# Other SBUF start addresses, modulo 512 bytes, for the stationary operands of a split-fp32 transformer kernel

## The chip, the cores and the metric

The kernel runs on one core of one Trainium2 chip. The metric is the device time of one execution in microseconds (us); lower is better. Times given for a kernel are the median of several executions with their lowest and highest.

## What is computed

The reference runs two transformer blocks, one after the other, on 256 tokens of width 1024, all in fp32. The first block normalises x, projects it; of the columns q, k and v go to a differential attention of 8 heads, u to a causal depthwise convolution of 31 taps, and g to two gates; then it has an FFN with 2816 inner columns. The second block has a stick-breaking attention, a linear recurrence and an FFN with 4096 inner columns. Cut to the dense products, which are what the change is about:

```python
# first block
proj = rms_norm(x, attn_norm_w) @ w_in                    # 1024 x 7168: q, k, v, u, g
y_a = attention(q, k, v) @ w_proj_attn                    # 1024 x 1024
y_b = silu(layer_norm(conv(u))) @ w_proj_conv             # 1024 x 1024
x = x + (g_a * y_a + g_b * y_b) @ w_out                   # 1024 x 1024
gt, up = split(rms_norm(x, ffn_norm_w) @ w_gate_up)       # 1024 x 5632
x = x + (silu(gt) * up) @ w_down                          # 2816 x 1024
# second block
proj = rms_norm(x, norm1_g_2) @ w_in_2                    # 1024 x 2560
x = x + concat(attention_2, lru) @ w_out_2                # 1024 x 1024
x = x + square(relu(rms_norm(x, norm2_g_2) @ w_up_2)) @ w_down_2   # 1024 x 4096, 4096 x 1024
```

## The kernel before, in words

**Numbers in two parts.** Every dense product is made of three matmuls. A weight w and an activation x are each kept as a high part (fp32r, the format in which TensorE reads it in one pass) and a low part (what the high part leaves): x_hi·w_hi + x_hi·w_lo + x_lo·w_hi. The activation part is the stationary operand (128 x 128: 128 rows of the contraction, 128 tokens), the weight part is the moving one (128 x 512).

**Units.** All weights are cut into units of four row blocks of 128 by 512 columns (1 MB), 120 of them (two have only two row blocks), in the fixed order of `weight_chunks`. For each unit SyncE's queue loads `raw` (three buffers, L428, or L409 for the first two), ScalarE copies it to `w_hi` (L589, L594), and VectorE (L928, L933) or, for units 7 to 27, GpSimd (L574) writes `w_lo` = raw - w_hi. `w_hi` and `w_lo` have three buffers each. TensorE then runs the unit, one row block j after the other and for each the two token tiles t, with these three matmuls (L1640, L1641, L1642; in the very last unit L1625 to L1627 with the loops turned round):

```python
x_h = hi[:, k0 + j, P * t:P * (t + 1)]
x_l = lo[:, k0 + j, P * t:P * (t + 1)]
nc.tensor.matmul(o, x_h, w_hi[:, slot, j, :], start=begin_, stop=False)
nc.tensor.matmul(o, x_h, w_lo[:, slot, j, :], start=False, stop=False)
mm = nc.tensor.matmul(o, x_l, w_hi[:, slot, j, :], start=False, stop=end_)
```

A unit is 4 x 2 x 3 = 24 such matmuls. `parts(c)` picks the stationary pair: `h_hi, h_lo` for the products that read a normalised x (and for `w_proj_conv`), `y_hi, y_lo` for `w_proj_attn`, `w_out` and `w_out_2`, `m_hi, m_lo` for the two down projections. The order of the work is written out by hand: small work of TensorE (transposes through `turn`, L1325; attention scores, L1370 and L1403; probabilities times v, L1387; suffix sums, L1414 to L1418; recurrence gates, L1439 and L1440) is put between units or in the middle of one. VectorE also runs the 31-tap convolution (L972) in the first 200 us.

**Places in SBUF.** Buffers are laid out by hand with `place` and `sb` (L152 to L160), at byte offsets in each partition. `w_hi` and `w_lo` take 24,576 bytes each, `h_hi` and `h_lo` 8,192, `m_hi` and `m_lo` 32,768. `y_hi` and `y_lo` lie on `m_hi`'s memory, and so do `gates` and `x_in` behind them (L217); `m_lo` and the first block's working buffers share the region behind `m_hi`. Slices inside a weight buffer step by 2,048 bytes, and the stationary slices by 512 (t) and 1,024 (j). All these sizes are multiples of 512, and so, in the kernel before, each of the six activation parts and each slice of them starts at the same address modulo 512 bytes as each weight slice: a distance of 0. Counted from `w_hi`, modulo 512, other buffers start at: `q_t`, `k_t`, `v_tok`, `gates`, `x_in`, `q2_t`, `k2_t`, `ff_m`, `neg_tri` 0; `wr_g`, `wi_g`, `w2_t` 160; `lru_u` 64; `raw`, `conv`, `x_res`, `ln_r` 64; `ident` and `mean_w` 192; `tok` 320; `a_tok`, `probs_t`, `glu` 448.

Of the kernel before, what the change touches and what calls it, by code (L numbers as in the profile page):

```python
# [9 lines left out]
F32R = mybir.dt.float32r  # L10
# [4 lines left out]
P = 128  # L15
D = 1024
S = 256
NT = S // P
EPS = 1e-6
KT = D // P  # L20
CW = 512
UK = 4
# [21 lines left out]
FK2 = FF2 // P  # L44
# [39 lines left out]
def build(nc, a, out):  # L84
# [19 lines left out]
    RAW, SPLIT = 3, 3  # L104
# [44 lines left out]
    with ExitStack() as ctx:  # L149
        cursor = [(nc.sbuf_base + 31) // 32 * 32]  # L150

        def place(name, shape, dt=F32, at=None):  # L152
            size = int(np.prod(shape[1:])) * 4
            if at is None:
                at = cursor[0]
                cursor[0] += (size + 31) // 32 * 32
            return nc.alloc_sbuf_tensor_at(name, shape, dt, offset=at), at

        def sb(name, shape, dt=F32, at=None):
            return place(name, shape, dt, at)[0]  # L160
# [2 lines left out]
            return ctx.enter_context(nc.semaphore(name))  # L163


        w_hi = sb("w_hi", [P, SPLIT, UK, CW], F32R)
        w_lo = sb("w_lo", [P, SPLIT, UK, CW], F32R)

        h_hi = sb("h_hi", [P, KT, S], F32R)
        h_lo = sb("h_lo", [P, KT, S], F32R)  # L170

        m_hi, m_at = place("m_hi", [P, FK2, S], F32R)
        y_hi, y_at = place("y_hi", [P, KT, S], F32R, at=m_at)
        qk_square = sb("qk_square", [P, NT, CW], at=y_at)
        y_lo = sb("y_lo", [P, KT, S], F32R, at=m_at + 4 * KT * S)

        region = cursor[0]
        m_lo = sb("m_lo", [P, FK2, S], F32R)
        ff_m = sb("ff_m", [P, NT, 256])
        ff_s = sb("ff_s", [P, NT, 256])  # L180
# [15 lines left out]
        glu_t, at = place("glu_t", [P, KT, PAD + S])  # L196
# [16 lines left out]
        ln_r, at = place("ln_r", [P, S])  # L213
        conv_sum = sb("conv_sum", [P, S], at=at)
        region_end = max(region_end, cursor[0])

        cursor[0] = m_at + 4 * (FK2 // 2) * S  # L217
        gates, x_at = place("gates", [P, NT, 2 * D])
        x_in = sb("x_in", [P, NT, D], at=x_at)
        vecs = sb("vecs", [VROWS, D], at=x_at + 4 * NT * D)  # L220
# [7 lines left out]
        x2_tok, at = place("x2_tok", [P, NT, W2])  # L228
# [17 lines left out]
        conv, at = place("conv", [P, KT, S])  # L246
# [1459 lines left out]
```

## Time and profile before

| | before |
|---|---|
| median of 3 executions | 742.98 us (742.23 to 743.13) |
| the profiled execution's own time | 745.36 us |
| its span, first to last instruction | 743.6 us |
| mean granted TensorE clock | 0.998 |
| TensorE matmuls, busy | 729.4 us (98%), 3428 of them |
| weight loads (beside the matmuls) | 594.2 us (80%) |
| VectorE / ScalarE / GpSimd busy | 483.9 / 398.1 / 174.6 us |
| DMA traffic | 131.45 MB, mean 177 GB/s |

The median is 2.4 us below the profiled execution's own time, and that is 1.8 us above its span. The busy time of TensorE counts each matmul from its start to a modelled end; matmuls overlap, so the distance from one start to the next, which the timeline shows, is what a matmul costs in a row of them.

### The profile page before, as it was taken

To read this page: it belongs to the slowest core of one execution; us is meant where nothing else is said; L and a number is where in the kernel's file an instruction comes from. 1 tells how busy PE (TensorE), PEld (TensorE's weight loads), DVE (VectorE), ACT (ScalarE), POOL (GpSimd) and SP (SyncE) were. 2 spreads that over 40 slices of the span, in tenths; PEclk is the share of its full clock that TensorE was granted. 3 is DMA by queue.
4 is the path that set the end of the run, shared out by engine and by line. 5 is a ranking of instruction groups with operands and counts; after the bars stand their busy time and mean duration, and the time that the engine had idled before them with its cause. 6 is when DMAs were issued, how large, how long until landed. Compare 5 with 4: busy or idle time off the path is not lost.

```text
span 743.6 us, 9120 instructions
## 1 busy us (share of the span) xinstructions
PE 729.4 (98%) x3428; PEld 594.2 (80%) x3428; DVE 483.9 (65%) x671; ACT 398.1 (54%) x526; POOL 174.6 (23%) x127
## 2 busy tenths in 40 slices
PE   7998999999999999999999999999999999999998
PEld 6786777777778888888888888888788888888886
DVE  4697988889987665555556454677866565653531
ACT  6744666655694464444445255569945555444330
POOL 1089799998310003000000000150001000000000
PEclk9999999999999999999999999999999999999999
DMA  8965445355547547566564555642354556455540
GB/s 287 258 208 183 126 159 197 115 199 169 170 154 265 181 137 227 171 188 200 178 186 170 196 198 170 227 130 97 114 177 164 177 170 207 170 182 192 203 142 29
DMA packets 82803, 131.45 MB, mean 177 GB/s; under 512 B 3988, under 2 KB 35804, under 8 KB 82760
## 3 DMA queue, kind: packets, MB, share of 16 engines
q1 hardware_dynamic: 82224, 129.61, 53.5%
q0 software_dynamic: 528, 1.25, 0.6%
q8 instruction: 28, 0.46, 0.3%
q14 instruction: 15, 0.12, 0.0%
q10 hardware_dynamic: 8, 0.02, 0.0%
HBM read 129.61 MB, written 1.25 MB: 176 GB/s over the span
## 4 chain that ended last, share of the span: by engine, by line
PE 70%; DVE 10%; POOL 9%; ACT 5%; issue 2%; DMA 2%; SPq 1%; ACTq 0%; POOLq 0%; DVEq 0%
PE acc L1640 21%; PE acc L1642 21%; PE acc L1641 21%; POOL w_lo L574 5%; DVE aux L972 5%; PE aux L1325 3%; DMA raw<-w_in_dram 2%; POOL qk_r L479 2%; ACT w_hi L589 1%; DVE w_lo L928 1%; POOL probs L546 1%; POOL qk_ss L491 1%; POOL probs L548 1%; DVE gates L1131 1%; SPq L409 0%
## 5 line engine op out<-in xcount | busy, mean ns | idle before, releaser
L928 DVE TENSOR_TENSOR w_lo<-raw,w_hi 128x2048 fp32r<-128x2048 f32 (+1 forms) x97 | 220.1, 2269 | 127.8 <-ACT w_hi L589 127.8
L589 ACT ACTIVATE w_hi<-raw 128x2048 fp32r<-128x2048 f32 x118 | 223.7, 1900 | 143.1 <-PE acc L1642 139.3
L1640 PE MATMUL acc<-w_hi,h_hi 128*128 128x512 f32 x640 | 257.5, 402 | 4.4 <-DVE tok L983 2.5
L1642 PE MATMUL acc<-w_hi,h_lo 128*128 128x512 f32 x640 | 251.2, 392 | 0.0
L1641 PE MATMUL acc<-w_lo,h_hi 128*128 128x512 f32 x640 | 250.4, 391 | 0.0
L1640 PEld LDWEIGHTS acc<-w_hi,h_hi 128*128 128x128 f32 x640 | 121.1, 189 | 30.6 <-DVE tok L983 3.1
L1642 PEld LDWEIGHTS acc<-w_hi,h_lo 128*128 128x128 f32 x640 | 120.7, 189 | 26.1
L1641 PEld LDWEIGHTS acc<-w_lo,h_hi 128*128 128x128 f32 x640 | 121.0, 189 | 23.2
L574 POOL TENSOR_TENSOR w_lo<-raw,w_hi 128x2048 fp32r<-128x2048 f32 x21 | 98.0, 4671 | 0.8 <-ACT w_hi L589 0.7
L972 DVE SCALAR_TENSOR_TENSOR aux<-glu_t,vec_t,aux 128x256 f32<-128x256 f32 x232 | 94.0, 481 | 0.0
L479 POOL TENSOR_TENSOR rstd<-ms,nhalf 128x2 f32<-128x2 f32 x4 | 8.7, 2183 | 339.9 <-DVE ms L955 339.9
L1640 PE MATMUL acc<-w_hi,m_hi 128*128 128x512 f32 x208 | 81.2, 390 | 0.0
L1642 PE MATMUL acc<-w_hi,m_lo 128*128 128x512 f32 x208 | 81.0, 389 | 0.0
L1641 PE MATMUL acc<-w_lo,m_hi 128*128 128x512 f32 x208 | 80.9, 389 | 0.0
L1640 PEld LDWEIGHTS acc<-w_hi,m_hi 128*128 128x128 f32 x208 | 39.0, 188 | 8.1
L1642 PEld LDWEIGHTS acc<-w_hi,m_lo 128*128 128x128 f32 x208 | 39.0, 188 | 8.1
L1641 PEld LDWEIGHTS acc<-w_lo,m_hi 128*128 128x128 f32 x208 | 39.0, 188 | 8.0
L616 ACT ACTIVATE m_hi<-aux 128x512 fp32r<-128x512 f32 x27 | 15.3, 598 | 54.5 <-PE aux L1325 54.5
L1640 PE MATMUL acc<-w_hi,y_hi 128*128 128x512 f32 x96 | 38.6, 402 | 0.9 <-DVE y_lo L1023 0.9
L1642 PE MATMUL acc<-w_hi,y_lo 128*128 128x512 f32 x96 | 37.5, 391 | 0.0
L1641 PE MATMUL acc<-w_lo,y_hi 128*128 128x512 f32 x96 | 37.4, 390 | 0.0
L947 DVE TENSOR_TENSOR m_lo<-aux,m_hi 128x512 fp32r<-128x512 f32 x27 | 17.9, 687 | 16.9 <-ACT m_hi L616 16.8
(219 smaller groups left out, 646.0 us busy)
## 6 DMA issues: line engine op xcount, KB each, us to landing
raw<-w_in_dram SPq DMA_DIRECT2D x30, 1024.0 KB, 5.2
raw<-w_down_dram SPq DMA_DIRECT2D x26, 1024.0 KB, 5.0
raw<-w_gate_up_dram SPq DMA_DIRECT2D x44, 512.0 KB, 4.8
raw<-w_up_dram SPq DMA_DIRECT2D x16, 1024.0 KB, 5.5
raw<-w_out_dram SPq DMA_DIRECT2D x8, 1024.0 KB, 5.0
raw<-w_in_dram SPq DMA_DIRECT2D x12, 512.0 KB, 4.6
raw<-w_proj_attn_dram SPq DMA_DIRECT2D x4, 1024.0 KB, 5.0
raw<-w_proj_conv_dram SPq DMA_DIRECT2D x4, 1024.0 KB, 5.1
```

Source lines behind the costliest of these rows:

```text
L479: nc.gpsimd.tensor_tensor(out_, in_, nhalf[:, 0:in_.shape[1]], ALU.pow).then_inc(s_out, 1)
L491: nc.gpsimd.tensor_scalar(part, part, 1.0 / HD, qk_e[:, st, t:t + 1], ALU.mult, ALU.add)\
L574: nc.gpsimd.tensor_tensor(w_lo[:, u % SPLIT, 0:nk, :], raw[:, u % RAW, 0:nk, :], f(w_hi[:, u % SPLIT, 0:nk, :]), ALU.subtract).then_inc(w_ ...
L589: nc.scalar.activation(w_hi[:, u % SPLIT, 0:nk, :], raw[:, u % RAW, 0:nk, :], ACT.Copy)\
L616: nc.scalar.activation(dst[:, 2 * g:2 * g + 2, :], aux[:, bank, :].rearrange("p (a b) -> p a b", a=2), ACT.Copy, scale=scale).then_inc(s_o ...
L928: nc.vector.tensor_tensor(w_lo[:, u % SPLIT, 0:nk, :], raw[:, u % RAW, 0:nk, :], f(w_hi[:, u % SPLIT, 0:nk, :]), ALU.subtract).then_inc(w_ ...
L947: nc.vector.tensor_tensor(lo[:, 2 * g:2 * g + 2, :], aux[:, bank, :].rearrange("p (a b) -> p a b", a=2), f(hi[:, 2 * g:2 * g + 2, :]), ALU ...
L972: nc.vector.scalar_tensor_tensor(out=conv_acc(ct) if tap < TAPS - 1 else conv[:, ct, :], in0=glu_t[:, ct, tap:tap + S], scalar=vcol(R_CONV ...
L1325: return nc.tensor.transpose(out_, in_, ident[:, :])
L1640: nc.tensor.matmul(o, x_h, w_hi[:, slot, j, :], start=begin_, stop=False)
L1641: nc.tensor.matmul(o, x_h, w_lo[:, slot, j, :], start=False, stop=False)
L1642: mm = nc.tensor.matmul(o, x_l, w_hi[:, slot, j, :], start=False, stop=end_)
```

## The change

The weights' parts stay where they are. Each of the six activation parts gets a start of its own modulo 512 bytes, counted from `w_hi`: `h_hi` 64, `h_lo` 256, `m_hi` 320, `y_hi` 384, `y_lo` 192, and `m_lo` 448 (it is the first buffer of the region). Gaps of less than 512 bytes are left between buffers. `gates`, `x_in`, `q2_t` and what lies with them now begin right behind `y_lo` (192). The region and all behind it move up by 960 bytes, so that, modulo 512, they stand 64 lower than before: `q_t`, `k_t`, `v_tok`, `ff_m` 448, `wr_g`, `w2_t` 96, `lru_u` 0, `raw`, `x_res`, `ln_r` 0, `ident` 128, `tok` 256, `a_tok`, `probs_t` 384. No instruction is added, removed or moved, and no wait changes.

```diff
-        w_hi = sb("w_hi", [P, SPLIT, UK, CW], F32R)
+        w_hi, w_at = place("w_hi", [P, SPLIT, UK, CW], F32R)
         w_lo = sb("w_lo", [P, SPLIT, UK, CW], F32R)
 
-        h_hi = sb("h_hi", [P, KT, S], F32R)
-        h_lo = sb("h_lo", [P, KT, S], F32R)
-
-        m_hi, m_at = place("m_hi", [P, FK2, S], F32R)
-        y_hi, y_at = place("y_hi", [P, KT, S], F32R, at=m_at)
+        def apart(at, off):
+            return at + (w_at + off - at) % 512
+
+        h_hi, at = place("h_hi", [P, KT, S], F32R, at=apart(cursor[0], 64))
+        h_lo, at = place("h_lo", [P, KT, S], F32R, at=apart(at + 4 * KT * S, 256))
+
+        m_hi, m_at = place("m_hi", [P, FK2, S], F32R, at=apart(at + 4 * KT * S, 320))
+        y_hi, y_at = place("y_hi", [P, KT, S], F32R, at=apart(m_at, 384))
         qk_square = sb("qk_square", [P, NT, CW], at=y_at)
-        y_lo = sb("y_lo", [P, KT, S], F32R, at=m_at + 4 * KT * S)
-
-        region = cursor[0]
+        y_lo, at = place("y_lo", [P, KT, S], F32R, at=apart(y_at + 4 * KT * S, 192))
+        gates_at = at + 4 * KT * S
+
+        region = apart(max(m_at + 4 * FK2 * S, gates_at + 4 * 2 * NT * D), 448)
+        cursor[0] = region
         m_lo = sb("m_lo", [P, FK2, S], F32R)
...
-        cursor[0] = m_at + 4 * (FK2 // 2) * S
+        cursor[0] = gates_at
         gates, x_at = place("gates", [P, NT, 2 * D])
```

## Rows read from the trace of the kernel before

**Rows 1.** The page: engines' busy time, and the granted clock by slices.

```profile
PE 729.4 (98%) x3428; PEld 594.2 (80%) x3428; DVE 483.9 (65%) x671; ACT 398.1 (54%) x526; POOL 174.6 (23%) x127
...
PEclk9999999999999999999999999999999999999999
```

**Rows 2.** Waits of TensorE and of the two splits; groups of instructions with idle time before.

```profile
PE acc L1640 <- DVE w_lo L928: 0.4, 1, 0.4
...
L589 ACT ACTIVATE w_hi<-raw 128x2048 fp32r<-128x2048 f32 x116 | 221.6, 1914 | 136.1 <-PE acc L1642 132.3 <-DMA raw<-w_in_dram 3.8
...
DVE w_lo L928 <- ACT w_hi L589: 127.8, 68, 5.1
```

**Rows 3.** Groups of TensorE's instructions: shapes, count | busy us, mean ns | idle.

```profile
L1640 PE MATMUL acc<-w_hi,h_hi 128*128 128x512 f32 x640 | 257.5, 402 | 4.4 <-DVE tok L983 2.5 <-DVE h_lo L941 1.5 <-DVE w_lo L928 0.4
...
L1640 PE MATMUL acc<-w_hi,m_hi 128*128 128x512 f32 x208 | 81.2, 390 | 0.0
...
L1640 PE MATMUL acc<-w_hi,y_hi 128*128 128x512 f32 x96 | 38.6, 402 | 0.9 <-DVE y_lo L1023 0.9
...
L1625 PE MATMUL acc<-w_hi,m_hi 128*128 128x512 f32 x8 | 3.1, 389 | 0.0
```

**Rows 4.** Timeline of TensorE, 48 matmuls in a row of the first down projection.

```profile
419.79 0.39 PE L1640 MATMUL acc<-w_hi,m_hi 128*128 128x512 f32 x1
...
430.45 0.39 PE L1642 MATMUL acc<-w_hi,m_lo 128*128 128x512 f32 x1
```

**Rows 5.** Timeline of TensorE behind a break, in the up projection.

```profile
599.51 0.47 PE L1640 MATMUL acc<-w_hi,h_hi 128*128 128x512 f32 x1
599.83 0.40 PE L1641 MATMUL acc<-w_lo,h_hi 128*128 128x512 f32 x1
...
600.30 0.39 PE L1640 MATMUL acc<-w_hi,h_hi 128*128 128x512 f32 x1
...
601.68 0.39 PE L1640 MATMUL acc<-w_hi,h_hi 128*128 128x512 f32 x1
```

**Rows 6.** Timeline of TensorE: gates of the recurrence and attention scores, plain fp32.

```profile
492.56 0.60 PE L1439 MATMUL aux<-lru_u,wr_g 128*128 128x256 f32 x2
...
495.58 0.59 PE L1440 MATMUL aux<-lru_u,wi_g 128*128 128x256 f32 x2
...
530.07 0.71 PE L1403 MATMUL aux<-q_t,k_t 64*128 64x256 f32 x4
530.61 0.39 PE L1405 MATMUL aux<-q_t,k_t 64*128 64x128 f32 x4
```

**Rows 7.** Groups of TensorE: three kinds of transposes.

```profile
L1325 PE MATMUL aux<-ident,tok 128*128 128x128 f32 x112 | 14.9, 275 | 1.0 <-DVE probs L1106 0.7 <-DVE tok L983 0.3
...
L1325 PE MATMUL aux<-ident,ff_m 128*128 128x128 f32 x44 | 6.6, 272 | 0.0
L1325 PE MATMUL aux<-ident,x_res 128*128 128x128 f32 x48 | 6.3, 273 | 0.2 <-DVE x_res L1159 0.2
```

**Rows 8.** Groups of weight loads (PEld).

```profile
L1640 PEld LDWEIGHTS acc<-w_hi,h_hi 128*128 128x128 f32 x640 | 121.1, 189 | 30.6 <-DVE tok L983 3.1 <-issue 2.1 <-DVE h_lo L941 1.9
...
L1440 PEld LDWEIGHTS aux<-lru_u,wi_g 128*128 128x128 f32 x8 | 1.5, 190 | 0.2
```

**Rows 9.** Groups of VectorE with two inputs in SBUF.

```profile
L928 DVE TENSOR_TENSOR w_lo<-raw,w_hi 128x2048 fp32r<-128x2048 f32 x95 | 217.6, 2291 | 123.3 <-ACT w_hi L589 123.3
...
L1246 DVE TENSOR_TENSOR h_lo<-conv,h_hi 128x1024 fp32r<-128x1024 f32 x2 | 2.4, 1222 | 0.8 <-ACT h_hi L868 0.8
L1019 DVE TENSOR_TENSOR conv<-conv,ln_r 128x1024 f32<-128x1024 f32 x2 | 2.4, 1218 | 0.0
```

**Rows 10.** Busy time by stretch: us, PE, PEld, DVE, ACT, POOL, clock, DMA share, GB/s.

```profile
100.00:200.00 100.00, 98.71 (x486) 76.97 (x485) 87.21 (x205) 61.19 (x131) 88.01 (x54) 1.00 0.51 167
...
600.00:700.00 100.00, 100.00 (x462) 83.09 (x462) 55.05 (x42) 45.43 (x39) 0.00 (x0) 1.00 0.55 189
```

**Rows 11.** Groups of TensorE, first 200 us alone.

```profile
L1640 PE MATMUL acc<-w_hi,h_hi 128*128 128x512 f32 x224 | 92.9, 415 | 4.4 <-DVE tok L983 2.5 <-DVE h_lo L941 1.5 <-DVE w_lo L928 0.4
```

## The prediction

> **What bounds the kernel now.** I read the page first: TensorE's matmuls are busy for 98% of the span, and its clock is granted in full in every slice [rows 1], so neither another engine nor the clock is the limit. Next the waits. TensorE's wait for the low part of the weights comes to 0.4 us in all; ScalarE, which makes the high part, waits 132.3 us for TensorE to give buffers back and only 3.8 us for transfers; VectorE waits 127.8 us for ScalarE [rows 2]. Whoever feeds TensorE is early. The groups of matmuls say what it does: 640 + 208 + 96 + 8 = 952 times the first of three matmuls with 512 columns, 1920, 648 and 288 of them on h, m and y, 2856 in all [rows 3]. Their mean of some 390 to 402 ns is a modelled length, so I took what one costs in a row from the timeline: 48 of them start between 419.79 and 430.45, which is 10.66 us over 47 steps, 226.8 ns each [rows 4]. 2856 x 226.8 ns is 647.7 us, 87% of the span of 743.6 us. The kernel is a stream of one kind of matmul, and the change can move the time by more than a microsecond or two only through this step.
>
> **Is there something in a step to win or lose?** Two views say that the step is not a constant of nature. Behind a break, the first step takes 320 ns (599.51 to 599.83), the next two together 0.47 us, so 235 ns each, and the eight from 599.83 to 601.68 on average 231 ns; only then does it settle [rows 5]. So the step depends on how one instruction stands in time to its neighbours. And plain fp32 matmuls, which run in two passes, go faster per pass: 14 steps from 492.56 to 495.58 are 215.7 ns each [rows 6], although each has its own weight load, as long as the others' (190 against 189 ns) [rows 8]. Between 226.8 and 215.7 lie 11.1 ns. In each step the array reads 512 elements of the moving part and meanwhile loads the next 128 x 128 stationary part. If these two readings disturb each other in SBUF, and if how much depends on their addresses modulo 512 bytes, then the change acts on 2856 steps. Before, the distance is 0 everywhere.
>
> **The change part by part.**
>
> *The instructions.* None is added, removed or moved, in no queue, SP's and GpSimd's included, and no wait is new. The edit costs what different addresses cost, and nothing else.
>
> *The 2856 matmuls.* No row of the trace has an fp32r matmul of 512 columns at another distance, so this price is bounded. Below, a step can fall to 215.7 ns: 2856 x 11.1 ns = 31.7 us less. Above, the slowest pair behind a break (235 ns) gives 8.2 ns more a step, 23.4 us more. Which value do the nearest rows speak for? The recurrence gates have their stationary part at 160 and their moving part at 64; the scores of the second attention have both at 0, the distance of the big matmuls. If a shared distance of 0 hurt, the scores should show it: their first four instructions (two pairs, the two of a pair on different halves of the rows) take 0.54 us from 530.07 to 530.61 [rows 6], and with 0.32 us for the first pair, the price of a first step behind a break [rows 5], the second pair takes 0.22 us, the gates' 215.7 ns within the last digit shown. The transposes have `ident` as the moving part at 192 and their stationary part at 320, 0 or 64; they take 275, 272 and 273 ns [rows 7]. Nothing here moves with the distance. These rows read the moving part at half the speed or for 128 columns only, so they don't settle it, but they are the only ones in which the distance varies. I take 0 for the change of a step.
>
> *The three steps of a break.* The eight steps behind a break cost 231 instead of 227 ns, some 35 ns, and the timeline has some 80 such breaks: 2.8 us in all. Another distance could lengthen or shorten this. Bounds: 2.8 us less to 2.8 us more; I take 0.
>
> *The split on ScalarE, VectorE and GpSimd.* `raw` goes from distance 64 to 0 against `w_hi`. Rows with two SBUF inputs exist at both distances: 1222 ns at 64 (`conv` and `h_hi`), 1218 ns at 0 (`conv` and `ln_r`), same size [rows 9]. So the 95 splits of 2291 ns on VectorE move by at most 4 ns per 1024 elements, 95 x 8 ns = 0.8 us of busy time. It costs the end nothing: VectorE idles 123.3 us before these splits [rows 9]. If that cover were gone the price would be this 0.8 us. The transfers into `raw` start 64 bytes from where they did, counted modulo 512; a slower one is hidden behind the 132.3 us that ScalarE waits for TensorE, and 3.8 us is all that it waits for transfers [rows 2]. Both cost 0.
>
> *Sum.* 745.4 us, the profiled execution's own time, plus 0 is 745.4 us; the median of the executions stands 2.4 us below that, so I forecast 743.0 us. An effect of 0.2%, 1.5 us, is about what a measurement of this kernel can tell from no change.
>
> One page of the notes speaks against the change. The Trainium skill, "TensorE: Matmul & The Clock Gate", in the part on what happens when a matmul is issued, says that TensorE reads moving and stationary operands through two independent SBUF ports, so that loading weights takes no reading speed from a running matmul. By that the addresses would not matter and the sum would be 743.0 us as well; by the bound of 215.7 ns it would be 711. The same page puts a warm step of 512 columns at N/2.4 + 2.5 ns, about 216 ns; the trace agrees for the plain fp32 passes and disagrees by 11 ns for the fp32r ones, so one of the two statements does not hold here.
>
> **The rivals.**
>
> *1. Faster: distance 0 is a collision.* Stationary and moving part begin at the same place modulo 512 in every step, and the moving stream is held up by the load. The new distances clear it. For it: 11.1 ns a step that the load alone doesn't explain, and a step that depends on relative timing behind a break [rows 4 to 6]. Against it: the scores at distance 0. Price by buffer: h, at 64 and 256, 1920 x 11.1 = 21.3 us; m, at 320 and 448, 648 x 11.1 = 7.2 us; y, at 384 and 192, 3.2 us. In the first 200 us lie 3 x 224 = 672 of h's [rows 11], 7.5 us, and there VectorE and GpSimd are 87% and 88% busy [rows 10]. The 14 us or so that each has free in 100 us would be enough for a gain of 4%, but the convolution is late next, and part may be lost. With all of it 743.0 - 31.7 = 711 us; with the early part lost 719 us; with y alone 740 us. Its middle is some 725 us.
>
> *2. Slower: a new distance settles at a longer step.* A step now ends in a favourable position, which it finds some eight steps behind a break. If the other distances never find it, each step stays at the 231 ns of the approach: 2856 x 4.2 ns = 12.0 us, 755 us; if it stays at the worst pair's, 766 us. It decides from a mean step above 227.3 ns on (1.5 us over 2856). For it: the steps of 231 and 235 ns in the timeline [rows 5]. Against it: these also happen at distance 0, so what sets them may not be the address.
>
> *3. The change doesn't do what it says.* All three matmuls of a triple have weight slices at 0, and `w_hi` and `w_lo` are the same distance from each other as before. If the conflict is one of successive moving reads, the homes of x, y and m don't touch it, and the time is 743.0 us. I count this with the forecast.
>
> **How the numbers follow.** Forecast, no effect, with rival 3 in it: 0.38; its own range is 741.5 to 744.5. Rival 1: 0.36, because 11 ns a step are there to be explained and the change touches every step. Rival 2: 0.26, because a position that is good by chance is as easily left. The likeliest case gives the time. For the range I add from the others until about 0.2 is left out: down to 718, which takes in rival 1 but for its full price, and up to 758, which takes in rival 2 with the 231 ns step (0.38 + some 0.28 + some 0.16). Faster by over 0.2%, 0.36; within 0.2%, 0.38; slower by over 0.2%, 0.26.
>
> **What would show it.** The timeline of the first down projection: 48 matmuls in 10.66 us means no effect; 10.14 us would be rival 1 in full, 10.86 us rival 2 at 231 ns. If only some distances matter, h, y and m will have different steps: read one stretch of each, and compare the step during which an h_lo (256) or m_lo (448) is loaded with the others of its triple. The length of VectorE's split should stay at 2291 ns within 10. The prediction is wrong if the step on h differs by more than 0.5 ns from 226.8, and wrong in its reason if the step is the same and the time moves all the same.

## The result and the profile after

The changed kernel takes 753.01 us (752.28 to 754.83, 3 executions) against 742.98 us before; the ratio is 1.0144, with a 95% interval of 1.0122 to 1.0166. It is slower by 10.0 us, or 1.4%.

The page of the changed kernel, the parts that answer to [rows 1] (all line numbers are 5 higher behind the edit: L1640 is now L1645):

```profile
span 753.1 us, 9120 instructions
...
PE 741.7 (98%) x3428; PEld 594.4 (79%) x3428; DVE 484.4 (64%) x671; ACT 398.1 (53%) x526; POOL 173.4 (23%) x127
...
PEclk9999999999999999999999999999999999999999
```

The same instructions, the same work on the other engines within 1.2 us each, the same clock in every slice, and 12.3 us more on TensorE (741.7 against 729.4). So the time went into the matmuls themselves. The groups that answer to [rows 3], and the split that answers to [rows 9]:

```profile
L1645 PE MATMUL acc<-w_hi,h_hi 128*128 128x512 f32 x640 | 260.1, 406 | 3.4 <-DVE tok L988 1.9
...
L1645 PE MATMUL acc<-w_hi,m_hi 128*128 128x512 f32 x208 | 82.0, 394 | 0.0
...
L1645 PE MATMUL acc<-w_hi,y_hi 128*128 128x512 f32 x96 | 39.3, 409 | 0.8 <-DVE y_lo L1028 0.8
```

```profile
L933 DVE TENSOR_TENSOR w_lo<-raw,w_hi 128x2048 fp32r<-128x2048 f32 x95 | 217.6, 2291 | 126.2 <-ACT w_hi L594 126.2
```

VectorE's split is unchanged to the nanosecond (2291 ns), though `raw` moved against `w_hi`. The timeline gives what a matmul costs in a row. Of the changed kernel, 96 steps of the first down projection, and 30 steps of the up projection:

```profile
407.28 0.39 PE L1645 MATMUL acc<-w_hi,m_hi 128*128 128x512 f32 x1
...
429.55 0.39 PE L1645 MATMUL acc<-w_hi,m_hi 128*128 128x512 f32 x1
...
608.79 0.40 PE L1645 MATMUL acc<-w_hi,h_hi 128*128 128x512 f32 x1
...
615.79 0.40 PE L1645 MATMUL acc<-w_hi,h_hi 128*128 128x512 f32 x1
```

22.27 us over 96 steps are 232.0 ns on m, and 7.00 us over 30 are 233.3 ns on h, where [rows 4] had 226.8. Note how little the other views show of this: no new wait, no gap, and a busy share of 98% both times. The mean of a group rises by 4 to 7 ns (402 to 406 on h, 390 to 394 on m, 402 to 409 on y), but it is a mean of modelled lengths; the distance between starts is what a step costs.

**Where the 9.5 us of span come from.** I paired the two traces matmul by matmul, since they have the same 3428 in the same order, and took the differences of the steps. Steps of ordinary length (under 260 ns) on h cost 8.7 us more, on m 3.3 and on y 1.3: 13.3 us. Three things give some of it back. Steps that contain a wait or follow a break are 1.6 us shorter, because a slower TensorE waits less for the others; the small matmuls are 0.8 us shorter; and one piece, 1.4 us, is an accident of this one execution's clock. The kernel before waits 2.5 us for `tok` in its early part, and behind it the granted clock is at 1.2 GHz for a moment. Busy times by stretch, the kernel before, then the changed one:

```profile
60.00:65.00 5.00, 5.00 (x18) 3.93 (x19) 5.00 (x14) 0.24 (x1) 5.00 (x2) 0.66 0.13 43
```

```profile
60.00:65.00 5.00, 4.60 (x24) 3.90 (x25) 5.00 (x14) 2.35 (x5) 4.99 (x3) 1.00 0.16 52
```

The column before the last two is the clock: 0.66 against 1.00. In the kernel before, seven matmuls there take some 427 ns, double the length; in the changed one the wait is 1.9 us and none of them does. A smaller piece goes the other way and is counted within the 1.6 us: at 10 us of the span, where the kernel before is at full speed, the changed kernel still has three steps of 0.42 to 0.58 us, and with the transposes beside them this costs it some 0.8 us. At the first product on y, which is at the end of the stretch in which VectorE and GpSimd are nearly full, the changed kernel is even ahead, by 0.7 us:

```profile
197.50 0.47 PE L1645 MATMUL acc<-w_hi,y_hi 128*128 128x512 f32 x1
```

(198.21 us before.) All of the net loss is made behind that point, where TensorE has hardly a wait: -0.7 + 10.2 us.

### The profile page after: what moved, and what is told of

Read it like the earlier page. It is cut to its first block, busy times and chain, and to the rows that moved or that the text cites. A ratio compares the mean times of both kernels' runs of the same rounds, so it can differ in the third digit from the quotient of the medians.

```text
span 753.1 us, 9120 instructions
## 1 busy us (share of the span) xinstructions
PE 741.7 (98%) x3428; PEld 594.4 (79%) x3428; DVE 484.4 (64%) x671; ACT 398.1 (53%) x526; POOL 173.4 (23%) x127
## 4 chain that ended last, share of the span: by engine, by line
PE 72%; DVE 12%; ACT 5%; POOL 5%; issue 2%; DMA 2%; SPq 1%; ACTq 0%; DVEq 0%; POOLq 0%
PE acc L1645 22%; PE acc L1647 22%; PE acc L1646 22%; DVE aux L977 7%; PE aux L1330 4%; DMA raw<-w_in_dram 2%; POOL w_lo L579 2%; POOL qk_r L484 2%; ACT w_hi L594 1%; DVE probs L1111 1%; POOL qk_ss L496 1%; DVE gates L1136 1%; DVE aux L973 1%; SPq L414 1%; DVE qk_ss L1129 0%
## 5 line engine op out<-in xcount | busy, mean ns | idle before, releaser
L1645 PE MATMUL acc<-w_hi,h_hi 128*128 128x512 f32 x640 | 260.1, 406 | 3.4 <-DVE tok L988 1.9
L1647 PE MATMUL acc<-w_hi,h_lo 128*128 128x512 f32 x640 | 253.9, 397 | 0.0
L1645 PEld LDWEIGHTS acc<-w_hi,h_hi 128*128 128x128 f32 x640 | 121.2, 189 | 31.8 <-DVE tok L988 2.3
L1645 PE MATMUL acc<-w_hi,m_hi 128*128 128x512 f32 x208 | 82.0, 394 | 0.0
L1645 PEld LDWEIGHTS acc<-w_hi,m_hi 128*128 128x128 f32 x208 | 39.2, 188 | 8.5
L1645 PE MATMUL acc<-w_hi,y_hi 128*128 128x512 f32 x96 | 39.3, 409 | 0.8 <-DVE y_lo L1028 0.8
```

## The experiments

Each is the changed kernel with other offsets or one line more. I name a distance as the kernel does, modulo 512 and counted from `w_hi`. For each run I give the settled step: the mean of all steps of 512 columns from the 13th of an unbroken stretch on, without those of 245 ns and more, taken from the trace for h, m and y. The kernel before has 226.8, 226.7 and 226.8 by this measure, the changed one 232.9, 231.9 and 233.4. With slightly other rules for what counts, the means of this and the other runs move by up to 0.4 ns on y, which has few such steps, and by 0.1 ns on h and m.

### Four theories of the cause

A: the distance between stationary and moving parts sets the step. B: what costs is that the high and the low part of a pair stand at different distances. C: the absolute addresses set it. D: the place of `raw` and of what lies behind it does.

**Uniform pairs, first set.**

```diff
-h_hi 64, h_lo 256, m_hi 320, m_lo 448, y_hi 384, y_lo 192
+h_hi 64, h_lo 64, m_hi 128, m_lo 128, y_hi 256, y_lo 256
```

> Both parts of each pair start at one and the same distance: h 64, m 128, y 256. Theory A (each load's distance from the moving weights sets the step): the step differs from 226.7 ns by buffer, each with its own value, and the time is not that of the kernel before. Theory B (what costs is that the high and the low part stand at different distances, so that successive loads jump): 226.7 ns for h, m and y and 743 us. Theories C (absolute addresses) and D (the place of raw and of the buffers behind it): some 233 ns everywhere, 753 us, if they explain the loss, since the rest lies about as after the change.

Measured: h 233.3, m 232.4, y 227.3 ns; 753.09 us, ratio 1.0143 (1.0128 to 1.0159). The mean on y holds some steps that are still settling; its stretches end at 226.7. B falls, since equal distances of a pair cost as much. D falls too, as the three buffers differ within one kernel while `raw` has one place. C is not settled here: it was expected to give one step everywhere, but the parts' absolute addresses differ between the buffers as much as their distances do.

**Uniform pairs, second set.**

```diff
-h_hi 64, h_lo 256, m_hi 320, m_lo 448, y_hi 384, y_lo 192
+h_hi 192, h_lo 192, m_hi 320, m_lo 320, y_hi 448, y_lo 448
```

> As the run before with other distances: h 192, m 320, y 448. Theory A: three more values of the step, one for each distance, different from one another. Theory B: 226.7 ns throughout, 743 us. C and D: as in the run before, the same step for all three buffers.

Measured: h 229.2, m 233.3, y 229.0 ns; 749.1 us, ratio 1.0084 (1.0067 to 1.0101). Three different values were expected; two came. By distance, so far: 192 and 448 agree, 64 and 320 agree, 256 is as good as 0. That the values repeat after 256 was not in any theory.

**Everything moved by 64 bytes.** All distances 0, as before the change:

```diff
-        cursor = [(nc.sbuf_base + 31) // 32 * 32]
+        cursor = [(nc.sbuf_base + 31) // 32 * 32 + 64]
```

> All buffers as in the kernel before, with distance 0, but everything moved up by 64 bytes, the weights too. Theories A, B and D: the step stays at 226.7 ns in the settled stretches and the time at 743 us. Theory C (absolute addresses modulo 512): the step changes, to some 233 ns.

Measured: 226.8, 226.7 and 226.8 ns; 741.53 us (one execution). The stationary parts stand here at the absolute addresses modulo 512 that h had in the first of these runs, and the step is the good one: C is out.

**The tail alone.** Distances 0, `raw` at 0 from the weights as in the changed kernel:

```diff
-        cursor[0] = region_end
+        cursor[0] = apart(region_end, 0)
         raw = sb("raw", [P, RAW, UK, CW])
```

> The six activation parts back at distance 0; only raw and the buffers behind it stand where the change put them modulo 512 (raw at 0 from the weights). Theories A, B and C: 226.7 ns and 743 us, nothing of the loss. Theory D: 233 ns, 753 us, or a longer split on VectorE than 2291 ns.

Measured: 226.8, 226.7 and 226.8 ns; 742.36 us, ratio 1.0003 (0.9989 to 1.0017), and the split on VectorE at 2290 ns. D is out for `raw` and what lies behind it; A is left.

### Is there a distance better than 0?

**Between the multiples of 64.**

```diff
-h_hi 64, h_lo 256, m_hi 320, m_lo 448, y_hi 384, y_lo 192
+h_hi 32, h_lo 32, m_hi 96, m_lo 96, y_hi 160, y_lo 160
```

> Uniform pairs at distances between the multiples of 64: h 32, m 96, y 160. The runs so far gave settled steps of 226.7 ns at 0 and at 256, 233.3 at 64 and at 320, 232.4 at 128, 229.0 at 192 and at 448. Theory A1 (the step is a smooth function of the distance modulo 256, with 0 its best): 32 and 96 lie between or near 227 and 233 ns, 160 near 230 ns, none below 226.7. Theory A2 (distance 0 is a partial collision, and a spot beside the multiples of 64 is free of it): one of the three falls well below 226.7 ns, towards the 215.7 ns of the plain fp32 passes.

Measured: h 233.3, m 234.3, y 233.4 ns; 755.91 us (one execution). Of the two versions of A put on record here, A2 (a place free of a partial collision, well below 226.7 ns) found nothing. A1 (a smooth function of the distance) was wrong as well: 32 bytes off already cost the full price, and 160 is 4 ns worse than 192.

**The other side, and the period.**

```diff
-h_hi 64, h_lo 256, m_hi 320, m_lo 448, y_hi 384, y_lo 192
+h_hi 224, h_lo 224, m_hi 384, m_lo 384, y_hi 352, y_lo 352
```

> h 224, m 384, y 352. If the law has a period of 256 bytes, m at 384 gives the 232.4 ns of 128, and y at 352 the value that 96 has in the run before. If the period is 512, they are new values. h at 224 (32 bytes short of the period): A1 says between 226.7 and 229 ns, A2 allows something well below 226.7.

Measured: h 233.4, m 232.7, y 234.3 ns; 755.39 us (one execution). 384 is like 128 (232.4) and 352 like 96 (234.3): the period is 256, as far as these pairs show it. At 224 nothing is gained.

**Distances below 32 bytes.** Each part becomes a view into a buffer that is 32 bytes longer:

```diff
+        def place_at(name, n, skip, at):
+            t, at = place(name, [P, n * S + 8], F32R, at=at)
+            return t[:, skip:skip + n * S].rearrange("p (k s) -> p k s", s=S), at
...
+        h_hi, at = place_at("h_hi", KT, 4, at=apart(cursor[0], 0))
```

> Distances that are no multiple of 32: h 16, m 248 (8 short of 256), y 4. If the step grows with the distance from 0 already within 32 bytes, 4 and 248 give 227 to 230 ns and 16 gives more. If it goes by 32-byte pieces, all of 0 to 31 behave as 0 and 248 as 224: h and y 226.7, m 233.3. If there is a spot better than 0, one of the three is below 226.7 ns, and it would beat both kernels.

Measured: h (16) 229.7, m (248) 233.3, y (4) 232.4 ns; 750.2 us (one execution). Four bytes from the good place cost 5.6 ns a step. None of the three expectations fits all of it: the step neither grows from 0 on nor goes by pieces of 32 bytes, and nothing beats 0. The 229.7 on h is no step that occurs: it is the mean of two kinds of stretches. Two neighbouring stretches of the up projection, 30 steps each:

```profile
604.26 0.39 PE L1650 MATMUL acc<-w_hi,h_hi 128*128 128x512 f32 x1
...
611.06 0.39 PE L1650 MATMUL acc<-w_hi,h_hi 128*128 128x512 f32 x1
...
616.10 0.40 PE L1650 MATMUL acc<-w_hi,h_hi 128*128 128x512 f32 x1
...
623.10 0.40 PE L1650 MATMUL acc<-w_hi,h_hi 128*128 128x512 f32 x1
```

6.80 us are 226.7 ns a step, 7.00 us are 233.3. The distances, instructions and shapes are the same in both. The weight slots rotate, but each of the three occurs with both steps, and every one of the up projection's stretches writes both halves of `acc`; so neither sets it. What is left as a difference is how the stretch was entered, which no run varied by itself. So a distance does not set a step directly. It goes with the steady rhythms that occur, and at 16 there are two.

Distance 16 is not alone in this. In the second set of uniform pairs, h at 192 has 228.9 ns in most stretches and 233.3 in two; of one of these, 30 steps in 7.00 us:

```profile
497.51 0.40 PE L1645 MATMUL acc<-w_hi,h_hi 128*128 128x512 f32 x1
...
504.51 0.40 PE L1645 MATMUL acc<-w_hi,h_hi 128*128 128x512 f32 x1
```

And the changed kernel itself, whose up projection has 233.3 ns on h, has 231.1 in the second block's projection, 36 steps in 8.32 us:

```profile
485.25 0.39 PE L1645 MATMUL acc<-w_hi,h_hi 128*128 128x512 f32 x1
...
493.57 0.39 PE L1645 MATMUL acc<-w_hi,h_hi 128*128 128x512 f32 x1
```

The 232.9 for h of the changed kernel and the 229.2 of distance 192 are therefore means of two kinds of stretches as well. At distances 0 and 256 the long stretches end at 226.7 ns, and no distance tried has a settled step below that.

**All at 0 or 256, in the changed layout.**

```diff
-h_hi 64, h_lo 256, m_hi 320, m_lo 448, y_hi 384, y_lo 192
+h_hi 256, h_lo 0, m_hi 0, m_lo 256, y_hi 256, y_lo 0
```

> The change as it was made, with its moved homes, gates and region, but with distances that are 0 or 256: h 256 and 0, m 0 and 256, y 256 and 0. If 256 bytes is the period and the distances modulo 256 are the whole cause, 226.7 ns everywhere and the time of the kernel before, 742 us. If the period is 512, or if unequal homes of a pair cost something, 230 ns or more and 746 us or more.

Measured: 226.7, 226.7 and 227.1 ns; 742.95 us against 743.0 us of the kernel before on the same chip, ratio 0.9998 (0.9985 to 1.0011). The same 96 steps as above, now 21.76 us:

```profile
400.70 0.39 PE L1645 MATMUL acc<-w_hi,m_hi 128*128 128x512 f32 x1
...
422.46 0.39 PE L1645 MATMUL acc<-w_hi,m_hi 128*128 128x512 f32 x1
```

The parts are laid out by the changed kernel's code, gaps and all, but each stands at 0 or 256, and the whole loss is gone. `gates` and `x_in` lie right behind `y_lo` as in the changed kernel, but at 0 instead of 192, and the region and `raw` stand at yet other places than in either kernel, so these were not held; no theory is left that needs them, since the step goes with the distance buffer by buffer in the runs above. The distances modulo 256 are the cause.

### Which two readings disturb each other?

**w_lo moved by 64 bytes.**

```diff
+        cursor[0] += 64
         w_lo = sb("w_lo", [P, SPLIT, UK, CW], F32R)
...
+h_hi 0, h_lo 0, m_hi 64, m_lo 64, y_hi 0, y_lo 0
```

> w_lo is moved 64 bytes away from w_hi; h and y stay at 0 from w_hi, m stands at 64 from w_hi and so at 0 from w_lo. Theory A with the load of the next stationary part as the partner of the running matmul: on h and y the matmuls with w_lo (L1646, during which the low part is loaded, 64 below them) get a step other than 226.7, and the triple costs more than 3 x 226.7 ns; on m the two matmuls with w_hi behave as at 64 and the one with w_lo as at 0, so the triple costs between 3 x 226.7 and 3 x 233.3 ns. If only the distance of a matmul's own two operands from w_hi's place counted, or that of the pair of moving reads did, h and m would have the same step.

Measured: h 231.9, m 234.5, y 232.1 ns; 752.13 us (one execution). The place of a moving part matters too: h's own parts are at 0 from `w_hi` as before the change, and the step is 5.2 ns longer. But m is not between 226.7 and 233.3: it is above both. On h the loss isn't confined to the matmul with `w_lo` either; its three steps average 231.0, 232.1 and 232.8.

**The loads lined up with the running moving part.**

```diff
+        cursor[0] += 64
         w_lo = sb("w_lo", [P, SPLIT, UK, CW], F32R)
...
+h_hi 0, h_lo 64, m_hi 0, m_lo 64, y_hi 0, y_lo 0
```

> w_lo 64 bytes from w_hi, as in the run with w_lo moved, but now h_lo and m_lo stand at 64 too, so that each load on h and m has distance 0 from the moving part that is being read while it is loaded; y stays at 0 and is the control. Theory L (the step is set by load against running moving read, nothing else): 226.7 ns on h and m, 232.1 on y as in the earlier run. Theory M (the jump from one moving part to the next, or a matmul's own two operands, counts): h and m stay near 232 ns.

Measured: h 231.2, m 231.3, y 232.0 ns; 749.9 us (one execution). The 96 steps on m, 22.18 us, 231.0 each:

```profile
403.52 0.40 PE L1646 MATMUL acc<-w_hi,m_hi 128*128 128x512 f32 x1
...
425.70 0.40 PE L1646 MATMUL acc<-w_hi,m_hi 128*128 128x512 f32 x1
```

Here every load stands at 0 from the moving part that is read while it runs, and still the step is 231. Theory L, load against running read and nothing else, falls. The jump of 64 bytes between two moving parts, that between two loads, or the distance of a matmul's own two operands has a part in it; the run doesn't part these three.

**One part of each pair.**

```diff
-h_hi 64, h_lo 256, m_hi 320, m_lo 448, y_hi 384, y_lo 192
+h_hi 0, h_lo 64, m_hi 64, m_lo 0, y_hi 0, y_lo 192
```

> w_lo back in place. Only one part of each pair is off distance 0: h_lo 64, m_hi 64, y_lo 192. Theory L with each load counted by itself: one load in three is off on h and y, two in three on m: h 228.9, m 231.1, y 227.4 ns on average. Theory P (what counts is the position that the whole sequence of loads falls into, so that one part that is off spoils the settled position of all): h and m at 230 ns or more, both, and h not much below m.

Measured: h 230.9, m 232.8, y 231.0 ns; 752.47 us (one execution). Counting each load by itself would give 228.9, 231.1 and 227.4. One part off in three spoils most of it, and a distance of 192, which alone costs 2.3 ns, costs 4.2 mixed with 0. What P forecast came (230 ns or more on both, h 1.9 below m). The three steps on h average 228.4, 229.1 and 235.7 ns: the long one is that of the matmul whose own stationary part is off (`h_lo`), not the one during which this part is loaded. That whole sequences fall into a rhythm of their own is the reading that fits; the run does not show how.

**Half the bytes in each load.** In the two down projections the stationary parts have 64 columns, so the products of the other 64 tokens of each tile are left out:

```diff
+                        pc = P // 2 if hi is m_hi else P
+                        o = acc_of(c, t)[0:pc, :]
+                        x_h = hi[:, k0 + j, P * t:P * t + pc]
+                        x_l = lo[:, k0 + j, P * t:P * t + pc]
```

> All distances 0. In the two down projections each stationary part has only 64 of its 128 columns, so half as many bytes are loaded during each matmul, while the moving part keeps its 512; the other half of the tokens is left out there. If the 11 ns a step above the plain fp32 passes are time that the load's reading takes from the moving stream, the step on m falls below 226.7 ns, to some 220; if they are a fixed cost of an fp32r matmul, it stays at 226.7 ns. h and y stay at 226.7 ns.

Measured: h 226.7, y 227.1 ns, and on m 230.0:

```profile
401.19 0.40 PE L1647 MATMUL acc<-w_hi,m_hi 128*64 128x512 f32 x1
...
423.27 0.40 PE L1647 MATMUL acc<-w_hi,m_hi 128*64 128x512 f32 x1
```

22.08 us over 96 steps. Both expectations missed. With half the bytes to load (a load takes 134 ns instead of 188) the step got longer, so the 11 ns above the plain fp32 passes are not time in proportion to the load. These matmuls also write 64 rows of the output instead of 128, so whether the shorter load or the smaller output lengthens the step is not parted. What the 11 ns are stays open.

## Why the prediction was right or wrong

- *The forecast and the range:* the forecast of 743.0 us (no effect, own range 741.5 to 744.5, chance 0.38) missed by 10 us. The time lies inside 718 to 758 only because that range held two opposite rivals beside the forecast; the one that happened had the least chance, 0.26. The prediction's own sign of being wrong, a step on h more than 0.5 ns from 226.8, came: 232.9.
- *What bounds the kernel, and that the change acts only through the step:* right. The ordinary steps cost 13.3 us more; what else moved (waits, small matmuls, the clock) gave 3.8 us back.
- *"I take 0 for the change of a step":* this is the term that failed. It was read from plain fp32 matmuls and transposes, which showed no effect of the distance [rows 6, 7]. Those rows read their moving part at half the speed or for 128 columns. The text said that they don't settle it, and chose by them all the same. The traces give +5.2 ns on m, +6.1 on h and +6.6 on y for fp32r matmuls of 512 columns.
- *The range and its upper rival:* rival 2 is what happened, a new distance that settles at a longer step. Its price from the eight steps behind a break (231 ns, 755 us) was near: 232 to 233 ns settled, and 753.0 us. The idea behind it, a step that never finds the good position, fits the run with distance 16, where the same distances give 226.7 or 233.3. That the size came out near is in good part luck: 231 ns is a mean of unsettled steps at distance 0, no run ties it to the settled steps at others, and these go, for uniform pairs, from 228.9 to 234.3. The argument against it, that slow steps also happen at distance 0 and so the address may not set them, was half true: at distance 0 they don't last, elsewhere they do.
- *Rival 1, distance 0 is a collision:* wrong. With the experiments, distances 4, 16, 248 and all multiples of 32 have been run up to 256 and several beyond, and no settled step is below 226.7. Distance 0 (or 256) is the best of them. None of them comes near the 215.7 ns of [rows 6]. That bound was also read too closely: those passes have 256 columns and the big matmuls 512, so the equality with the time that the prediction quotes for 512 columns is one of nanoseconds, not of speed, and no row shows 215.7 ns as the floor of a 512-column step.
- *Rival 3, the change doesn't do what it says:* wrong: the homes of the stationary parts alone made the 10 us. Whether the places of the moving parts among each other count as well is not shown; moving `w_lo` cost 5.2 ns on h, but it also moved `w_lo` away from the stationary parts.
- *"The three steps of a break", taken as 0:* the mean of the 2nd to 9th step behind a break went from 230.2 to 232.8 ns. In the first 200 us, where stretches have 12 steps, this makes the loss smaller: 2.2 us on 587 steps there, against 6.5 us on 1215 steps of h later. The prediction's bound of 2.8 us less to 2.8 us more held: some 80 breaks x 8 x 2.6 ns = 1.7 us, where it took 0.
- *The split and the transfers, 0:* right, 2291 ns before and after.
- *The early stretch:* the text saw VectorE and GpSimd at 87% and 88% as a thing that could swallow a gain. They swallowed part of the loss instead: TensorE's waits shrank. That a half-clock moment of 1.4 us fell away beside this belongs to the two executions that were traced.
- *The comparison within a triple, which the prediction asked for:* in the changed kernel the step during which `h_lo` (256) is loaded averages 230.8 ns, the other two 233.6 and 234.3; on m the step with the load of `m_lo` (448) has 228.9, the others 231.2 and 235.5. The load that stands better has the shorter step here, but it is not back at 226.7, and in the run with one part of each pair moved it is the other way round.
- *The two read ports:* The Trainium skill, "TensorE: Matmul & The Clock Gate", in its part on issuing a matmul, says that TensorE has two independent SBUF read ports. The prediction concluded that the addresses would not matter; the measurement is against that conclusion, 226.7 against 231.9 to 233.4 ns. Whether a load takes reading time from the running matmul is not shown either way: with half the bytes to load, the step grew to 230.0 ns.

## What to carry to other kernels

In this kernel a row of fp32r matmuls with 512 columns, each with its own load, has a rhythm, and the start addresses of stationary and moving operands modulo 256 bytes decide which ones it can settle into: keep all of them, slices included, at the same place modulo 256 (here worth 1.4%). Other types, widths and rows that keep one stationary part were not tried. To see it, divide the time between the first and the last start of a long stretch by the number of steps; busy shares and waits showed nothing here. And when rows of another form say that a parameter doesn't matter, ask whether they run at the rate of the ones that count.

## What the runs showed of the hardware that was not expected

- The settled step by uniform distance: 0 and 256: 226.7 ns; 192 and 448: 229.1 (mostly 228.9); 128 and 384: 232.4 and 232.7; 32, 64, 160, 224, 248, 320: 233.3 to 233.4; 96 and 352: 234.3; 4: 232.4; 16: 226.7 or 233.3. Five pairs that are 256 apart agree within 0.3 ns, and moving everything by 64 bytes changed nothing.
- 226.7 ns and 233.3 ns are 544 and 560 cycles of the 2.4 GHz that were granted there; at distance 16 both occur in one execution with the same distances, and so do 228.9 and 233.3 at 192, and 231.1 and 233.3 in the changed kernel.
- Stationary parts of 64 columns instead of 128 made a step longer: 230.0 against 226.7 ns.
- Open: which pair of readings the distance acts through. The load against the running moving part is not enough (231.2 ns with all of these at 0), and a matmul's own two operands, the jump between moving parts and the jump between loads were not tried apart.
